# The half rotation of queries and keys made by small transfers and a column of signs, where a matmul with a permutation made it

## The reference

```
z = rms_norm(x) @ w_in;  q, k, v, ... = split(z)
q = partial_rope(rms_norm(q), positions);  k = partial_rope(rms_norm(k), positions)

x1, x2 = xr[..., :8], xr[..., 8:16]          # only 16 of 64 features turn
rot = concat(x1*cos - x2*sin, x2*cos + x1*sin)
```

## Time and profile before

| | |
|---|---|
| median of three runs | 1692.95 us |
| profiled execution | 1695.31 us, its span 1693.5 us |
| PE busy | 1638.5 us (97%) |
| DVE, ACT, POOL busy | 63%, 37%, 57% |
| run of twelve jobs up to the first attention step | 286 to 356 us |
| runs of six jobs | 411 to 454, 509 to 550, 605 to 647 us |

### The profile page before, as it was taken

One profiled execution on the slowest core, in us unless ns is written; L12 is line 12 of the kernel. 1 busy time (PEld: TensorE's weight loads), 2 busy tenths in 40 slices (PEclk: granted clock), 3 DMA queues, 4 the chain that ended last, 5 costly groups with the idle time before them and its releaser, 6 DMA issues. The chain is left out here.

```text
span 1693.5 us, 29231 instructions
## 1 busy us (share of the span) xinstructions
PE 1638.5 (97%) x11306; PEld 1548.2 (91%) x11306; DVE 1063.5 (63%) x1640; ACT 619.1 (37%) x1303; POOL 965.3 (57%) x687
## 2 busy tenths in 40 slices
PE   7999999999999999999899899999999999999999
PEld 4899989988889898898898889999999999998998
DVE  7777774963856556677889678333333334869685
ACT  4354533233342434433334334333333333433242
POOL 4656552321312222287785716877777777786876
PEclk9999999999999999999999999999999999999999
DMA  4111112233113131345541512222243222373734
GB/s 166 50 51 62 62 56 100 67 78 113 53 56 102 56 107 64 103 155 201 178 153 51 194 62 76 101 76 76 76 159 108 76 76 76 137 263 114 257 141 147
DMA packets 72764, 182.12 MB, mean 108 GB/s; under 512 B 14704, under 2 KB 26416, under 8 KB 72000
## 3 DMA queue, kind: packets, MB, share of 16 engines
q1 hardware_dynamic: 51376, 159.13, 26.8%
q10 hardware_dynamic: 21264, 21.27, 4.2%
HBM read 131.36 MB, written 49.28 MB: 107 GB/s over the span
## 5 line engine op out<-in xcount | busy, mean ns | idle before, releaser
L573 PE MATMUL bank<-xh,wsh 128*128 128x264 f32 x2170 | 622.9, 287 | 22.4 <-POOL wsl L549 6.7
L573 PE MATMUL bank<-xh,wsl 128*128 128x264 f32 x2170 | 618.6, 285 | 0.0
L573 PE MATMUL bank<-xl,wsh 128*128 128x264 f32 x2170 | 618.0, 285 | 0.0
L573 PEld LDWEIGHTS bank<-xh,wsh 128*128 128x128 f32 x2170 | 410.4, 189 | 26.1 <-issue 18.1
L573 PEld LDWEIGHTS bank<-xl,wsh 128*128 128x128 f32 x2170 | 410.6, 189 | 0.3
L573 PEld LDWEIGHTS bank<-xh,wsl 128*128 128x128 f32 x2170 | 410.5, 189 | 0.0
L573 PE MATMUL bank<-acth,wh 128*128 128x352 f32 x984 | 329.3, 335 | 4.7 <-POOL actl L511 3.8
L573 PE MATMUL bank<-acth,wl 128*128 128x352 f32 x984 | 319.9, 325 | 0.0
L573 PE MATMUL bank<-actl,wh 128*128 128x352 f32 x984 | 318.6, 324 | 0.0
L499 POOL TENSOR_SCALAR wh<-wraw 128x512 fp32r<-128x512 f32 x104 | 86.0, 827 | 382.4 <-PE bank L573 371.9
L549 POOL TENSOR_TENSOR wsl<-praw,wsh 128x512 fp32r<-128x512 f32 (+1 forms) x157 | 243.8, 1553 | 84.1 <-ACT wsh L1153 83.9
(11 more groups left out here) (170 smaller groups left out, 2394.8 us busy)
## 6 DMA issues: line engine op xcount, KB each, us to landing
praw<-in_weights SPq DMA_DIRECT2D x34, 1024.0 KB, 4.9
wraw<-in_weights SPq DMA_DIRECT2D x52, 512.0 KB, 3.3
h_scratch<-ev SPq DMA_DIRECT2D x44, 264.0 KB, 2.1
acc<-h_scratch SPq DMA_DIRECT2D x4, 2112.0 KB, 12.3
ev<-x_scratch SPq DMA_DIRECT2D x6, 1056.0 KB, 5.0
spare<-x_scratch SPq DMA_DIRECT2D x6, 1056.0 KB, 5.1
praw<-in_weights SPq DMA_DIRECT2D x8, 768.0 KB, 4.7
ta_scratch<-tg ACTq DMA_DIRECT2D x24, 176.0 KB, 1.9
```

What stands on the lines that cost most here:

```text
L573: return nc.tensor.matmul(*args, **kw)
```

## The change

The matmul with `perm` and its semaphore are gone. A tile `qrot` (two buffers of 128 x 352) is zeroed once. After each copy into `qsb`, ACT waits until the copy has landed and issues four transfers, each of 8 partitions x 352, which swap rows 0 to 7 with rows 8 to 15 of both heads. DVE reads `qrot`, a column `sign` (-1, +1, else 0, made once from `perm`) and the sine in one instruction with two multiplications.

```
-                wait(pe, rot_used, base + k)
-                mm(aux1[:, 0:BW], perm, qsb[:, k % 2, :], start=True, stop=True).then_inc(rot_done, 1)
...
-                wait(act, rot_done, base + k - 1)
+                wait(act, ss_done, base + k - 1)
+                wait(act, rot_in[k % 2], swapped(base + k - 2))
                 wait(act, t1_done, base + k - 1)
                 f(qsq[:, k % 2, :], bank[job.bank][:, 0:BW], ACT.Square)
                 f(qsb[:, k % 2, :], bank[job.bank][:, 0:BW], ACT.Identity, scale=gain).then_inc(free[job.bank], 1)
+                if base + k == 0:
+                    act.wait_ge(zeros_done, 1)
+                wait(act, rot_used, base + k - 1)
+                act.wait_ge(free[job.bank], job.after)
+                for h in range(2):
+                    for lo, hi in ((0, ROT // 2), (ROT // 2, 0)):
+                        act.dma_start(qrot[h * HD + lo:h * HD + lo + ROT // 2, k % 2, :],
+                                      qsb[h * HD + hi:h * HD + hi + ROT // 2, k % 2, :]).then_inc(rot_in[k % 2], 16)
...
-                wait(dve, rot_done, base + k + 1)
+                wait(dve, rot_in[k % 2], swapped(base + k))
                 wait(dve, rope_done, base + k)
-                V.tensor_tensor(rt2[:, :], aux1[:, 0:BW], cs[:, 1, x], ALU.mult).then_inc(rot_used, 1)
+                stt(rt2[:, :], qrot[:, k % 2, :], sign[:, 0:1], cs[:, 1, x], ALU.mult, ALU.mult).then_inc(rot_used, 1)
...
+            V.memset(qrot[:, :, :], 0.0).then_inc(zeros_done, 1)
+            vec(V.tensor_reduce(sign[:, :], perm, AX.X, ALU.add))
+            vec(V.tensor_scalar(sign[:, :], sign[:, :], -1.0, None, ALU.mult))
             dve.wait_ge(cs_loaded, 16)
```

More of the change, by code:

```diff
@@ L339, in build @@
             qsq = tensor(s, "qsq", [P, 2, BW])
+            qrot = tensor(s, "qrot", [P, 2, BW])
+            sign = tensor(s, "sign", [P, 1])
             pt = tensor(s, "pt", [P, 2, 2 * P])
@@ L447, in build @@
         v_stored, kv_stored, cs_loaded = [sem(f"v_stored{i}") for i in range(2)], sem("kv_stored"), sem("rope_loaded")
-        ss_done, rot_done, std_done = sem("qk_sumsq"), sem("qk_rotated"), sem("qk_std")
+        ss_done, std_done = sem("qk_sumsq"), sem("qk_std")
+        rot_in, zeros_done = [sem(f"halves_swapped{i}") for i in range(2)], sem("rotation_zeros")
         rot_used, t1_done, rsum_done, rrec_done, rope_done = (
@@ L475, in build, with swapped @@
         block = ctx.enter_context(nc.Block())
+        def swapped(j):
+            return 16 * 4 * (j // 2 + 1)
         def wait(eng, s, value):
```

## The result

The changed kernel takes 1719.92 us (median; 1718.14 to 1722.32) against 1693.01 us of the kernel before on the same chip: a ratio of 1.0154, 95% interval 1.0141 to 1.0168, so it is slower by 1.5%. The forecast was 1694.7 with a range up to 1700.5. The profiled execution took 1718.14 us, its span is 1716.3, 22.8 more than before.

A forecast was written before the change was run, and what follows sets the result against it. PE, 97% busy, and DVE's rope chain were taken as nearly level, so saved PE time becomes waiting. Stretches of +0.6, +1.5, -0.2 and -0.2 gave +1.7 on 1692.95: 1694.7 us, range 1690.5 to 1700.5.

The forecast's parts named there:

- rival A: PE alone is the bound, so thirty removed matmuls take 17.7 us off: 1675; chance 0.10 with its smaller form.
- The landing of the swaps: Swap transfers land 1.8 us after issue; up to about 4 us this costs the rope nothing.
- rival C: Swaps land late in a queue behind loads of `vgr`, at 6.7 us: +8, 1701; chance 0.08.
- rival D: DVE's new instruction runs at half rate, each rope 0.37 us longer: +9.6, 1704; chance 0.04.
- Its exposure: DVE's new instruction can be stretched while POOL splits weights: 0.5 us for the twelve ropes, between 0 and 1.9.
- Four issues on ACT: Each job's four swap issues take ACT 1.8 us, between the copy and the root; bounds 0.8 and 2.4.
- rival B: Swap issues are dear, 0.6 us each on ACT, so PE stands longer: +6 to +8, 1699 to 1701; chance 0.18.
- Third and fourth run: In the last two runs of six, DVE's end sets the attention start: -0.2 us each, bounds -1.5 and +1.5.
- the forecast's stop of 1.6: In the third and fourth run PE stands 1.6 us before job 1's sum, waiting for ACT's root.
- the sum's +0.6, +1.5, -0.2 and -0.2: Forecast changes in us for the run of twelve and the second, third and fourth run, together +1.7.
- the last stop: At a run of six's last sum PE waits 1.4 to 1.5 us for ACT's root of job 4.
- the gains that were set against the stops: In the third and fourth run, six removed matmuls of 0.59 us each, set against PE stops of 1.6 and 1.5.

The follow-up runs named there:

- 3: The changed kernel with neither rotation matmul nor swaps, DVE's new instruction reading the unrotated copy: 1697.90 us, ratio 1.0023 to the kernel before.
- 4: The changed kernel without rotation matmul or swaps, DVE's rope also cut from five instructions to three: 1676.65 us, ratio 0.9892 to the kernel before.
- 1: The changed kernel with ACT's root moved ahead of the swap issues and group loads: 1699.80 us, ratio 1.0031 to the kernel before.
- 7: The kernel before, matmul still run, with only DVE's new instruction, reading the SBUF copy, in place of the old one: 1700.76 us, ratio 1.0034.
- 5: The changed kernel with 22 and 13 idle matmuls filling PE's two stops in each run of six: 1709.70 us, ratio 1.0092 to the kernel before.
- 2: The changed kernel with the swaps issued by SP between its weight loads, not by ACT: 1708.35 us, ratio 1.0081 to the kernel before.
- 6: The kernel before, matmul and old rope kept, plus the four swaps issued by ACT and read by nothing: 1717.35 us, ratio 1.0137.

## Why the prediction was wrong

**Right.** PE's 17.7 us could not be collected (3 and 4 show both halves of it), so rival A was rightly put low. The landing of the swaps costs nothing: 9.9 us before the first rope of each run, as for PE before; rival C is refuted, by 1 as well, where the swaps are issued at the same time after their copies and the kernel is 21 us faster. The instruction on DVE takes 585 ns in the median where 573 was read from the earlier trace rows; by the rule of half rate in the Trainium skill (Vector Engine (DVE) Microarchitecture Reference, section Points that are easy to get wrong) it would be about 0.9 us (an estimate), and the trace disagrees, so rival D is refuted. Its exposure was sized at 0.5 us for the twelve ropes; 7 gives some 1.2 us over all stages for the whole instruction, with more that the profile does not place. The places were right too: the sum of job 1 and the last sum are where PE stands. Two small sums of the forecast are off and change nothing: by its terms a rope is 4.59 us and not 4.57, and a run of six -0.3 and not -0.2.

**Wrong, the step "Four issues on ACT".** I priced them by stores of another form, 0.45 each, and called 0.6 the bound. They take 0.63 to 0.66, fixed, not by bytes: 2.65 us for 1.8. This is rival B's condition, whose time of 1699 to 1701 was itself 19 us too low, so the price is not all that failed.

**Wrong, the step "Third and fourth run".** It started ACT's copy of job 1 on time, 0.2 us behind PE. The issues of job 0 and the two loads behind them held ACT until 525.48, and the copy came 1.1 us late. I had counted the issues of one job between the copy and the root, and two jobs' stand there. With this the forecast's stop of 1.6 is 1.6 + 0.9 (issues) + 1.1 (late copy) + 0.1 (loads), 3.7 of the 3.9 measured. At two swaps, where issue and lateness are small, the stop is 1.39, and the four stretches of the profile differ from before by +1.6, +1.4, -0.9 and -0.3, near the sum's +0.6, +1.5, -0.2 and -0.2. The sum described a kernel with less in the queue. That is by one profile, whose span is +2.8; by the ratio of all runs the kernel is +6.8 (4.4 to 9.1), and where the other 4 us lie is open.

**Wrong, the last stop.** The 1.5 us there were put down to ACT's issues alone. 3 has none and stands 1.23 there, for DVE's chain: the forecast had the later of two causes for the only one.

**Missing, the clock.** No term of the sum, of B's price or of the range had it, and the rows that I had of PE in the runs of six were all at full clock. Some 8 to 11 of the 27 us are matmuls at the 1.2 GHz level behind stops of 2.3 us and more (5). At the forecast's own stops of 1.6 and 1.5 us the term might well have been zero: none of the stops of 1.03 to 1.67 us in the runs of six with two and three swaps has a fall behind it. It came in with the longer stops, so it follows from the two steps above. This is in part why the ratio grows faster than the issues: +0.4% at two, +0.8% at three, +1.5% at four.

**Also off: the gains that were set against the stops.** I took PE's coming 3.5 us early in each run of six as room for them. Stops add up on PE (3.9, 0.5 and 2.3 in the third run, 6.7 us), and 3.5 us of saved matmuls cannot cover that; the forecast had 1.6 and 1.5.

**What stays open.** The rope table is issued at 285.5 to 289.6 us in these kernels, with no edit ahead of it that would explain it, and it lands 5.6 to 8.5 us after its issue. Both are worth some 3 us, as much as the differences of 1, 3, 7 and the two-swap kernel from the kernel before. In the profile of 1 they are 2.6 and 2.9 of the 5.5 us that its span is longer (1699.0 for 1693.5), so there everything behind the first rope comes to nothing. Whether these four are truly slower by their own edits, or by that, the runs don't tell. Nor do they tell why the clock falls behind one stop and not behind another of the same length. Of the versions that compute everything none beat the kernel before.

## What to carry to other kernels

Here a transfer of 8 rows cost ACT 0.63 us to issue, for 352 columns as for 32. Read such a price from the trace of the same form of transfer, count it for every job whose issues stand ahead of the instruction that others wait for, and put that instruction (here the root) ahead of the issues. When the busiest engine is level with another one, a saving on it is worth nothing until the other is shortened too, while every new stop is paid in full. Where a forecast has the matrix engine standing for some us in the midst of dense work, put a term for the lower clock behind the stop into the sum's range: after the change it was 0 to 2.8 us a stop, for stops of 2.0 to 4.0 us.

## What the runs showed of the hardware

- An issue of a transfer of 8 rows from SBUF to SBUF on ACT's queue takes 631 ns at least and 632 in the median, for 352 columns as for 32 (on SP's queue in 2: 624 and 625). Stores of `kst` took 0.33 to 0.45.
- After the change, behind PE's stops of 2.3 to 3.9 us in the third run the matmuls start 0.29 us apart for 1.6 to 2.3 us of lost time; behind stops of 1.39 and 1.67 in the kernels with two and three swaps there is none. Length alone doesn't decide: behind 2.36 us after the change (second run), 3.34 in 2 and 3.29 in 6 the clock stayed at 1.00, behind 1.84 in 3 it fell to 0.83 over 10 us. Matmuls that compute nothing, put in the stops, kept the clock at 1.00 and made the kernel faster.
- The three-operand instruction on DVE with two fp32 sources in SBUF took 585 ns in the median for 352 columns (454 to 1399, L1446 after the change), the plain product of two such tiles 526 (L1452 before).
- The first rope behind a swap on SP's queue, issued 0.5 us after a load of 512 KB, waited 3.4 us longer than on ACT's queue; the loads of `kg` were issued ahead of it as well, so the cause is not separated.
